# VectorE's order at the norms of a two-block transformer: root and scaled values ahead of the last weight splits

## The reference, cut to what matters

```python
def first_block(...):
    for l in range(2):
        h = _rmsnorm(x, norm1_g[l]) * (1.0 + sc1) + sh1
        x = x + g1 * _mixer(h, ...)            # ends in  (...) @ w_out[l]
        h = _rmsnorm(x, norm2_g[l]) * (1.0 + sc2) + sh2
        x = x + g2 * _conv_ffn(h, ...)         # h @ w_up, conv, gate, @ w_down[l]
    return _rmsnorm(x, final_g)

def second_block(x, mem, ...):
    for l in range(2):
        h = rmsnorm(x, norm_pre[l])
        ...                                    # five branches of h; one reads
        mem_kv = rmsnorm(mem, mem_norm[l]) @ w_mem_kv[l]
        ...
        x = x + rmsnorm(merged @ w_out[l], norm_post[l])
    return x
```

## Time and profile before

| | |
|---|---|
| median of 3 runs | 1615.66 us (1615.60 to 1618.19) |
| the profiled execution | 1621.64 us, of it 1619.8 us between first and last instruction |
| TensorE busy | 1539.4 us, 95% |
| VectorE busy | 1149.2 us, 71% |
| ScalarE busy | 827.9 us, 51% |
| GpSimd busy | 56.5 us, 3% |
| mean granted TensorE clock | 0.979 of full speed |

### The profile page before, as it was taken

The page is one execution under the profiler, slowest core; times in us unless marked ns, Lnnn a source line. Parts: engine busy times, 40 slices in busy tenths (PEclk is TensorE's granted clock), DMA queues, the critical chain, the costliest instruction groups (busy, mean ns, idle before and its releaser), DMA issues. The chain is left out here.

```text
span 1619.8 us, 31315 instructions
## 1 busy us (share of the span) xinstructions
PE 1539.4 (95%) x12608; PEld 1464.3 (90%) x12608; DVE 1149.2 (71%) x2182; ACT 827.9 (51%) x1509; POOL 56.5 (3%) x60
## 2 busy tenths in 40 slices
PE   6999999999999998999999898999999799999997
PEld 4888899999988988999999898999899799999997
DVE  5656557788645666669996677877876678777774
ACT  3553545655535645447665564554455644644453
POOL 1000001000010000020002000000000100000000
PEclk9998999999999999999999999999999999999999
DMA  9643456566676442354554543444345342543430
GB/s 392 260 181 145 157 218 226 198 260 246 236 291 281 156 159 78 133 207 176 189 183 167 217 164 105 160 154 157 130 156 203 113 153 105 185 154 131 157 130 27
DMA packets 47407, 289.19 MB, mean 179 GB/s; under 512 B 9944, under 2 KB 11992, under 8 KB 12832
## 3 DMA queue, kind: packets, MB, share of 16 engines
q1 hardware_dynamic: 38880, 280.83, 46.7%
q10 hardware_dynamic: 8384, 6.36, 1.2%
HBM read 284.91 MB, written 2.26 MB: 177 GB/s over the span
## 5 line engine op out<-in xcount | busy, mean ns | idle before, releaser
L1975 DVE TENSOR_TENSOR w_lo<-ring,w_hi 128x1024 fp32r<-128x1024 f32 x436 | 526.8, 1230 | 273.8 <-ACT w_hi L1612 272.6
L1319 PE MATMUL bank<-h_hi,w_hi 128*128 128x256 f32 x2256 | 640.2, 291 | 8.8 <-ACT h_hi L1691 3.7
L1320 PE MATMUL bank<-h_hi,w_lo 128*128 128x256 f32 x2256 | 629.9, 287 | 0.0
L1325 PE MATMUL bank<-h_lo,w_hi 128*128 128x256 f32 x2256 | 582.4, 287 | 0.0
L1612 ACT ACTIVATE w_hi<-ring 128x1024 fp32r<-128x1024 f32 x436 | 447.7, 1053 | 110.2 <-PE bank L1325 109.9
L1319 PEld LDWEIGHTS bank<-h_hi,w_hi 128*128 128x128 f32 x2256 | 441.1, 196 | 22.5 <-issue 16.8
L1320 PEld LDWEIGHTS bank<-h_hi,w_lo 128*128 128x128 f32 x2256 | 441.3, 196 | 0.5 <-issue 0.5
L1325 PEld LDWEIGHTS bank<-h_lo,w_hi 128*128 128x128 f32 x2256 | 413.0, 196 | 0.3 <-DVE h_lo L1980 0.2
L1319 PE MATMUL bank<-a_hi,w_hi 128*128 128x256 f32 x352 | 99.8, 283 | 0.9 <-DVE w_lo L1975 0.6
L1320 PE MATMUL bank<-a_hi,w_lo 128*128 128x256 f32 x352 | 98.3, 279 | 0.0
L1325 PE MATMUL bank<-a_lo,w_hi 128*128 128x256 f32 x352 | 98.2, 279 | 0.0
(11 more groups left out here) (337 smaller groups left out, 2349.8 us busy)
## 6 DMA issues: line engine op xcount, KB each, us to landing
ring<-weights SPq DMA_DIRECT2D x266, 1024.0 KB, 4.9
pos_bias<-scratch ACTq DMA_DIRECT2D x4, 512.0 KB, 6.7
x<-x_t ACTq DMA_DIRECT2D x1, 1024.0 KB, 6.4
scratch<-line ACTq DMA_DIRECT2D x1, 1024.0 KB, 8.1
mem_x<-mem_t ACTq DMA_DIRECT2D x1, 1024.0 KB, 6.5
out_t<-x SPq DMA_DIRECT2D x2, 512.0 KB, 2.6
co<-const SPq DMA_DIRECT2D x1, 462.0 KB, 6.8
levels_f<-levels ACTq DMA_DIRECT2D x1, 448.0 KB, 12.6
```

The source lines that it names most:

```text
L1319: pe.matmul(to, WH[:, b % SPLIT, o, :], hi[:, k, :], start=(i == 0), stop=False)
L1320: pe.matmul(to, WL[:, b % SPLIT, o, :], hi[:, k, :], start=False, stop=False)
L1325: last = pe.matmul(to, WH[:, b % SPLIT, o, :], lo[:, k, :], start=False, stop=(i == n - 1))
L1975: ve.tensor_tensor(WL[:, b % SPLIT], ring_half(b), WH[:, b % SPLIT].bitcast(F32), ALU.subtract).then_inc(w_lo_v, 1)
```

## The change

Only VectorE's walk over the steps changes. From the second norm on (`begun`: a `norm` step was seen), a `root` step and the `stat` steps 6 and 7 no longer run splits, and a `root` or `norm` step does its own work first and runs `split_to` behind it (for `root` not at all). Steps of other kinds between them, `mod` among them, run their splits as before. No operation is added or removed; ScalarE's, TensorE's, GpSimd's and the loader's orders are the same.

```diff
+            begun = False
             for st in p.steps:
-                late = st.kind in ("wo1", "dn") and st.j >= KD - 2
+                late = st.kind in ("wo1", "dn") and st.j >= KD - 2 or st.kind in ("root", "norm") and begun
+                begun = begun or st.kind == "norm"
                 if late:
                     do[st.kind](st)
-                split_to(st.upto)
+                if not begun or not (st.kind == "root" or st.kind == "stat" and st.k >= KD - 2):
+                    split_to(st.upto)
                 if st.kind in do and not late:
                     do[st.kind](st)
```

## The result

| | before | changed |
|---|---|---|
| median of 6 runs each on one chip | 1615.63 us (1612.44 to 1618.19) | 1628.08 us (1624.12 to 1629.53) |
| ratio, 95% interval | | 1.0074 [1.0061, 1.0087] |
| profiled execution, its span | 1621.64, 1619.8 us | 1628.39, 1626.6 us |
| mean granted TensorE clock | 0.979 | 0.975 |

The direction was right; the size was not. The forecast was +7.3 us, the comparison gave +12.4 us, and 1628.1 us lies above the range's upper end of 1625.6.

What follows compares the result with a forecast made beforehand. TensorE, busy for 95% of the span, was taken as the bound. A 1.14 + B 1.14 + C 3.9 + clock 1.7 + D 0 - E 0.57 = +7.3 us on 1615.66 gave 1623.0 us; range 1620.0 to 1625.6.

Steps and rivals of the forecast that it cites:

- A and B: Norms behind w_out, layers 0 and 1, first block: the moved split delays `h_val` and TensorE, +1.14 us each.
- The longer gap buys no new one: At A and B a half-speed stretch is there already, so the longer waits add no clock loss.
- C: Norm of mem: three splits move behind it; TensorE's w_down tile 4 waits for the first, +3.9 us (2.8 to 5.0).
- The lead of the root: At C the root starts 1.08 us earlier; without that lead the cost there would be 5.0 us.
- D: Final norm: the root could start 0.71 us earlier, but TensorE's wait stays the same, 0 us.
- E: Norm behind w_out_2 of layer 0: the split holds up the root today, so moving it gains, -0.57 us.
- The clock: Behind the new gap at C, TensorE runs some 3.4 us at half speed, +1.7 us; other bound 0.
- One per gap is what the rows show: Argument against a second slow stretch: each TensorE gap has one half-speed stretch behind it.
- Rival 2: A second slow stretch, at C or at A or B: +1.7 us again, 1624.7 us; chance 0.12.
- Rival 1: No slow stretch behind C, since 1.93 us of idling left the clock at 1.00: 1621.3 us; chance 0.24.
- The range: 1620.0 to 1625.6 us: takes in rivals 1 and 2, plus 1.3 us below and 0.9 above for run spread.
- Faster rivals: Root leads at C, D and E (2.4 us) reach TensorE and one slow stretch goes (1.7): 1611.6 us; chance 0.03.

Runs made afterwards that it cites:

- the run with a wait of 1.02 us: Kernel before, changed at C only, with the first of three splits left ahead of the root and two behind the norm: ratio 0.9999 [0.9986, 1.0011].
- the last kernel: Kernel before with the changed order at D and E only, waits filled with constant products, five more before a second-block `h_val` wait: ratio 0.9958, 1608.67 us.

## Why the prediction was right in its steps and wrong in its sum

- **A and B, +1.14 each: right.** 2.99 us for 1.86, twice, and the split on the row between `rsq` and `h_val`. A and B alone gave 1.0019 [1.0000, 1.0038], which holds 2.3 us. "The longer gap buys no new one" holds too as far as traces go: a slow stretch stands behind 14 of 18 waits of 1.86 us and at 6 of 8 of 2.99 us.
- **C, +3.9: right.** 3.79 to 3.88 us in all six traces with a bare wait there. The lead of the root, 1.08 us, came as worked out, which is why it is not 5.0. What decides it is the first of three splits, by the run with a wait of 1.02 us.
- **D, 0, and E, -0.57: right.** 4.18 us as before; 5.09 to 4.53.
- **The clock, +1.7: the step that failed.** The term was too small: beyond its waits the change cost 4.7 ± 2.0 us, slow time rose by 5.3 ± 2.5, and filling C's wait alone gave back 5.7 with 3.4. "One per gap is what the rows show" was read from one trace, and priced as 3.4 us at C and nothing elsewhere. That a slow stretch goes with C's wait was right, in all six bare traces, and none goes with 1.02 us. But it was 3.4 us long in four of them and 6.8 in two. By their average of about 4.5 us, less what lies inside the wait, C loses about 2.1 us and not 1.7; D and E add about 0.8 us by their longer form (8 of 8 against 6 of 14), if that isn't chance. These two make 2.9 us of the 4.7 ± 2.0; where the rest of it stands, if it is there, no run shows. The Trainium skill, "TensorE: Matmul & The Clock Gate", Part 1 on the HAM clock gate, says that the number of slow products differs from run to run of one kernel. These traces agree, with 3.4 or 6.8 us at the same place. The prediction cited that rule, and then still priced the short form alone. Rival 2, a second slow stretch, was the nearest of the cases at 1624.7; it got 0.12 on the ground of that same one trace.
- **Rival 1's evidence was luck too.** The wait of 1.93 us at 646.70, behind which the clock stayed at 1.00, has a slow stretch in 9 of the 17 traces. The changed kernel's own is one of them:

```profile
644.48 1.97 PE L1489 MATMUL sums<-v_a,probs_t 128*128 128x64 f32 x8 [1.93 <-DVE probs_t L2270]
```

```profile
644.10:650.90 6.80, 6.42 (x30) 6.43 (x31) 3.55 (x6) 1.41 (x3) 0.00 (x0) 0.50 0.46 158
```

- **The range: too narrow for a reason of its own.** Its edges took the spread of three runs, 1.3 us below and 0.9 above. The runs of the kernel before scatter over 1610 to 1624 us (standard deviation 3). A median of six carries some 1.5 us of that, on each side of the comparison. The first comparison missed by 5.1 us, the pooled means by 2.9 ± 2.0, so some 2 us of the miss can be scatter; but the pooled mean of 1626.0 us still lies above the range.
- **Faster rivals: wrong, as weighed.** The leads at C and D reached nobody. E's did, by 0.56 us, and the last kernel has that order.

What stays open: whether C's wait lengthens the stretches at D and E, and what makes up the last 2 us or so of the clock's part, if they are there.

## What to carry to other kernels

Before moving work behind a long step of an engine that keeps strictly to its order, ask of every single piece who needs it first and when: here two of three splits could go behind 8 us of norm at no price that can be measured, and the third cost TensorE 3.8 us. A wait of some 4 us that left TensorE idle cost more than its length here (7.8 us bare, 2.1 filled). So read the slow stretch in several traces, take the long form into the range, and try filling it with products of constants. Where runs of one program scatter by 3 us, neither three runs nor a pair of profiled executions can size an effect of 5.

## What the runs showed of the hardware

- Filling TensorE's waits with products that nobody reads makes the kernel before 0.3% faster (0.9971 [0.9956, 0.9986] and 0.9970 [0.9957, 0.9983]). TensorE does more work and is done earlier.
- The slow stretches at C, D and E come in two lengths at one place, 3.4 or 6.8 us. The long ones begin 0.7 us or more before TensorE's wait is over, the short ones later (28 cases). C's wait of 1.02 us had none (2 traces), the 1.86 us of A and B had one in 14 of 18 cases, and C's 3.8 us always (6 traces).
- Slow time costs less than its size: over 115 runs of the kernel before 0.60 us of time (0.50 to 0.71) go with 1 us of it. In the changed kernel's stretch at E TensorE was busy for only 4.53 of 6.80 us, so there much of it falls into waits for other engines.
